# The new tokens' value product of the sample attention, contracted over 128 rows instead of 32

## What is computed

```python
def dilated_attention_sample(q, k_all, v_all, rel_bias):
    # q: (B,T,H,Dh) are the last T rows of k_all/v_all: (B,L,H,Dh)
...
    s = jnp.einsum('bthc,btkhc->bthk', q, kg)
    s = s * (HEAD_DIM ** -0.5) + bias.T[None, None]
    s = jnp.where(valid[None, :, None, :], s, NEG)
    p = jax.nn.softmax(s, axis=-1)
    return jnp.einsum('bthk,btkhc->bthc', p, vg)
```

## Time and profile before

| | us |
|---|---|
| median of 3 runs | 1195.9 (1193.57 to 1197.24) |
| span of the profiled execution, first to last instruction | 1191.4 |
| TensorE busy in it | 1134.9 (95%) |
| VectorE, ScalarE, GpSimd busy | 406.9, 323.6, 144.5 |
| share of the span on the chain that ended last | TensorE 85%, DMA 7%, VectorE 4% |

### The profile page before, as it was taken

How to read it: one execution, slowest core, us unless ns; L and a number is a source line. 1 busy time by engine, 2 the same in 40 slices (tenths; PEclk the granted TensorE clock), 3 DMA queues, 4 the chain that set the end, 5 groups by cost and what they waited for, 6 DMA issues and landing times.

```text
span 1191.4 us, 14847 instructions
## 1 busy us (share of the span) xinstructions
PE 1134.9 (95%) x5656; PEld 586.6 (49%) x5656; DVE 406.9 (34%) x968; ACT 323.6 (27%) x635; POOL 144.5 (12%) x141
## 2 busy tenths in 40 slices
PE   6999999899999999999999999899999988989997
PEld 3444443566666666655554555333443333334443
DVE  0232132556663242323256556362111111024443
ACT  2232231677741121110011111211111110134443
POOL 0110110011130000000011111321312210000000
PEclk9999999899999999999999999898999998989999
DMA  9211101311035525333568423799999999863421
GB/s 315 63 49 40 40 30 53 100 37 37 2 135 175 169 80 167 129 147 144 200 244 305 142 89 129 273 373 383 417 419 394 422 419 402 319 262 136 145 103 40
DMA packets 75061, 224.19 MB, mean 188 GB/s; under 512 B 18334, under 2 KB 32062, under 8 KB 60656
## 3 DMA queue, kind: packets, MB, share of 16 engines
q1 hardware_dynamic: 64384, 194.26, 44.0%
q0 software_dynamic: 9888, 26.37, 5.8%
q10 hardware_dynamic: 720, 2.62, 0.5%
HBM read 196.62 MB, written 31.32 MB: 191 GB/s over the span
## 4 chain that ended last, share of the span: by engine, by line
PE 85%; DMA 7%; DVE 4%; ACT 1%; issue 1%; POOL 0%; SPq 0%; ACTq 0%; POOLq 0%; DVEq 0%
PE pair L1915 14%; PE pair L2134 14%; PE pair L2331 11%; PE pair L2429 9%; PE pair L2197 9%; DMA R<-in_w_up 5%; PE pair L2353 4%; PE pair L1984 3%; PE pair L1971 3%; PE pair L1997 3%; PE pair L2226 1%; PE pair L2046 1%; PE pair L2318 1%; PE pair L2063 1%; PE pair L2050 1%
## 5 line engine op out<-in xcount | busy, mean ns | idle before, releaser
L2134 PE MATMUL pair<-R 128*128 128x352 f32 x576 | 180.8, 462 | 0.0
L1915 PE MATMUL pair<-R 128*128 128x512 f32 x384 | 172.0, 605 | 2.1 <-DMA R<-in_w_in 2.1
L2331 PE MATMUL pair<-R 128*32 128x512 f32 (+2 forms) x896 | 156.8, 628 | 11.2 <-DMA R<-in_w_up 9.2
L2134 PEld LDWEIGHTS pair<-R 128*128 128x128 f32 x576 | 105.3, 190 | 54.5 <-issue 4.4
L1915 PEld LDWEIGHTS pair<-R 128*128 128x128 f32 x384 | 73.3, 194 | 90.1 <-issue 90.1
L2429 PE MATMUL pair<-R 128*128 128x512 f32 x256 | 113.5, 601 | 1.7 <-issue 1.7
L2197 PE MATMUL pair<-R 128*128 128x512 f32 x256 | 113.8, 597 | 0.0
L2331 PEld LDWEIGHTS pair<-R 128*32 128x32 f32 (+2 forms) x896 | 50.0, 129 | 102.8 <-issue 98.5
L1736 DVE TENSOR_TENSOR R<-pair,R 128x256 f32<-128x256 f32 x21 | 8.9, 424 | 216.7 <-ACT R L1188 216.7
L2429 PEld LDWEIGHTS pair<-R 128*128 128x128 f32 x256 | 48.7, 193 | 60.7 <-issue 60.7
L2353 PE MATMUL pair<-R,bias 128*32 128x512 f32 (+2 forms) x448 | 76.4, 596 | 0.6 <-ACT bias L1192 0.6
(11 more groups left out here) (297 smaller groups left out, 1249.1 us busy)
## 6 DMA issues: line engine op xcount, KB each, us to landing
R<-in_w_gate SPq DMA_DIRECT2D x32, 1024.0 KB
R<-in_w_up SPq DMA_DIRECT2D x32, 1024.0 KB
R<-in_w_down SPq DMA_DIRECT2D x32, 1024.0 KB, 15.9
R<-in_x_prompt SPq DMA_DIRECT2D x16, 512.0 KB, 3.5
R<-in_cache_k SPq DMA_DIRECT2D x8, 1024.0 KB, 5.0
R<-in_cache_v SPq DMA_DIRECT2D x8, 1024.0 KB, 4.9
R<-y_dram SPq DMA_DIRECT2D x16, 512.0 KB, 6.7
R<-in_w_in SPq DMA_DIRECT2D x3, 2048.0 KB
```

Source lines behind the costliest of these rows:

```text
L1915: last = mm(bk[4 + part][0:n, :], xTs[a.u][:, c, 0:n], wA[:, c, AD * part:AD * part + AD], start=(c == 0), stop=(c == DC - 1))
L2134: last = mm(bk[b][:, 0:n], wB[q % 2][:, c, which, :], xT[:, c, lo:lo + n], start=(c == 0), stop=(c == DC - 1))
L2331: last = mm(bk[2 + u][r, :].rearrange("p (w f) -> p w f", w=2), xgT[u][:, c, r], wgu[s][:, :, c, :], start=(c == 0), stop=(c == DC - 1))
```

## The change

The last product of `weigh_values` contracts over all 128 rows. For that, the rows behind the 32 real ones must be zeros on one side and finite on the other: GpSimd clears the values' last tile at the start of the program, VectorE clears slot 7 of `PTs` once the prompt's attention is over, and two waits are adapted (`pool_set` counts one more). In the listing of the changed program every instruction behind the two new ones keeps its place and order on its engine.

```diff
@@ gpsimd, start of the program
         pool.memset(ones[:, :], 1.0).then_inc(S("pool_set"), 1)
         pool.memset(blank, 4 * TOK).then_inc(S("pool_set"), 1)
+        pool.memset(V[:, PT, :], 0.0).then_inc(S("pool_set"), 1)
@@ scalar, evac_qkv
             act.wait_ge(S("prj_full"), 3 * a.t + 3)
+            if n == SAMP:
+                act.wait_ge(S("pool_set"), 5)
             act.activation(V[0:n, a.t, :], bk[6][lo[2]:lo[2] + n, :], ACT.Copy).then_inc(S("prj_free"), 1)
@@ vector, keep_u
             if q == 0 and j == 0:
-                dve.wait_ge(S("pool_set"), 5)
+                dve.wait_ge(S("pool_set"), 6)
@@ vector, before the convolution
         dve.wait_ge(S("ot_full"), NSTEP)
         then(dve.memset(qbd, 0.0))
+        then(dve.memset(PTs[:, :, 7, :], 0.0))
         dve.wait_ge(S("qkT_done"), TILES)
@@ tensor, weigh_values
-            last = mm(bk[3][strips[3], :], rows(7, SAMP), V[0:SAMP, PT, :], start=False, stop=True)
+            last = mm(bk[3][strips[3], :], rows(7, P), V[:, PT, :], start=False, stop=True)
```

## The result

| | before | changed |
|---|---|---|
| median, us | 1193.57 (5 runs, 1189.19 to 1197.24) | 1184.05 (5 runs, 1180.12 to 1187.04) |
| ratio to before | 1 | 0.9921, 95% interval 0.9900 to 0.9943 |
| span of the profiled execution, us | 1191.4 | 1185.2 |
| TensorE busy in it, us | 1134.9 | 1125.6 |

The change makes the kernel faster by 0.79% (0.57 to 1.0%). The forecast was 0.65% and 1188.1 us.

The account below looks back on a forecast made before the run. TensorE's issued matmuls were taken to bound the kernel, busy 95% of the span. Eight calls at 0.97 us save 7.8 us, memsets and later stages cost nothing: 1195.9 - 7.8 = 1188.1 us, range 1184.5 to 1192.4.

Parts of the forecast that it names:

- The mechanism and its size: In `weigh_values`, the 128-row product starts beside the far products; each of eight calls saves 0.97 us, together 7.8 us.
- What was costed at nothing: GpSimd's memset at the start and VectorE's ahead of eight copies: hidden in idle time; uncovered, 0.6 and 0.1 to 0.7 us.
- the low bound of 0.1: VectorE's memset of 128 x 128: a quarter of 0.48 us is 0.1 us, at most 0.7.
- What so_full sets off: Loads after TensorE's calls stay in time: batch 7's values keep 22 us less 1.9, output weights 21.8 us.
- as argued: Experts' stage: its weight stream starts earlier by what TensorE gained, so the stage keeps its length and the gain isn't eaten.
- The step that failed: Final sum for the whole kernel: span 1191.4 - 7.8 = 1183.6 us; median kept 4.5 us above it, 1188.1.
- The lower end: Bottom of the forecast range for the whole kernel: 2.3 us of run spread and 1.3 us of clock below, 1184.5 us.
- The term of the saving: Eight calls of `weigh_values`, each 0.97 us shorter on TensorE: 7.8 us saved.
- The first, that the product does not join: In `weigh_values`, only one change of form goes, saving 0.8 us, time 1195.1 us; chance 7%.
- The second and third: Clock in the experts' stage: second, saving falls to 3.8 us, under 3.6 at 3%; third, over 3.6 us slower, 2%.

## Why the prediction was right about the change and wrong about the time

**The mechanism and its size were right.** Step by step: L2099 is 128*32 and starts with the far products, 0.02 us behind them (expected: within 0.05). A call takes 1.86 us in the timeline's rounding, 1.85 expected. From the first call to the last it is 117.12 us, 6.75 less than before (expected 6.8). The idle time ahead of its weight loads is gone. The stretch from the first call to the output projection is 7.7 us shorter, 8 x 0.97 = 7.8 expected. The form and the free strip were named as the two causes, and each was taken away alone: of the 0.97 us the form without the strip gives 0.13, the strip without the form nothing, and only both together give all.

**What was costed at nothing costs nothing that could be measured.** The memsets stand where expected, GpSimd's first and then VectorE's:

```profile
1.67 0.53 POOL L789 MEMSET R<- 128x512 f32 x1
10.74 1.03 POOL L793 COPY R<-R 128x1024 f32<-128x1024 f32 x1 [8.55 <-DVE R L1325]
```

```profile
349.77 0.17 DVE L1531 MEMSET R<- 128x128 f32 x1
...
356.56 0.18 DVE L1418 COPY R<-stT 128x16 f32<-128x16 f32 x1 [0.76 <-POOL R L834]
360.42 0.53 DVE L1422 TENSOR_TENSOR R<-pair,R 128x352 f32<-128x352 f32 x1 [3.68 <-PE pair L2138]
```

0.53 us of GpSimd's idle time and 0.17 us on VectorE, near the low bound of 0.1, with the same 0.76 and 3.68 us of idle time behind it as in the earlier trace rows. VectorE's stands at 349.8 instead of 346.9 us because everything from the projections on runs that much later in this execution. No wait of TensorE before the first score is new: the lines and what they wait for are those of before. Of the lengths the one that grew most, an idle time of 3.2 us at L1933 that was 1.8, is 3.2 in the kernel without the product and the memsets too.

**What so_full sets off stayed in time.** Batch 7's values and the output weights:

```profile
558.71 0.35 SPq L585 DMA_DIRECT2D R<-in_cache_v  x1
...
565.50 9.45 SPq L591 DMA_DIRECT2D R<-in_w_out  x8
```

From 558.71 to their first read at 578.87 it is 20.2 us (expected 22 - 1.9), from 565.50 to 587.27 21.8 us (expected 21.8). No wait came of it. Nothing shows that the experts' stage took any of the gain back, as argued: its length is 293.9 to 295.8 us in the changed traces, inside the 291.9 to 297.2 of before. Finer than that scatter the traces can't tell; the 8.1 us between the medians of 54 and 19 runs say that the gain arrived.

**The step that failed is the last one, "The median of the runs stands 4.5 us above the span; with that kept, it is 1195.9 - 7.8".** A run's time stands 1.8 us above its span, not 4.5: the profiled execution of the changed kernel has 1187.04 and a span of 1185.2, and the distance is 1.7 to 2.1 in every run of every kernel here. The 4.5 us that stand ahead of the prediction compared one execution's span with the median of others. So the profiled execution of before took some 1191.4 + 1.9 = 1193.3 us, and the three runs shown lay high in the kernel's scatter: 54 runs give 1192.8. From there the same saving leads to 1192.8 - 7.8 = 1185.0, against 1184.7 over 19 runs. Of the 4.05 us between forecast and measured median 3.1 are thus the base, 0.3 the saving (8.1 against 7.8) and 0.6 the luck of the five runs. The rest of the failure is the width: I took "2.3 us below and 1.3 above" of three runs for the scatter, where runs of before reach from 1187.7 to 1200.1. The lower end, 1188.1 - 2.3 - 1.3 = 1184.5, had no room for a high base and this scatter together, and 1184.05 falls 0.45 us outside. The term of the saving was right to 0.3 us.

**The rivals.** The first, that the product does not join, fell at once; the experiments on strip and rows show under which conditions it would have held. The second and third, a part or more given back, put the clock's scatter on the change; it exists, but in all kernels. The granted clock of the 54 runs of before goes from 0.974 to 0.987 and correlates with the time by -0.74; 0.001 of clock is worth 0.7 us. A share of the clock that moves like this between runs of one kernel belonged into the range, not into a rival.

## What to carry to other kernels

As far as these runs show it, for tiles of 128 x 32 in float32: products run side by side on TensorE when their tiles have the same form and stand on strips that are free. A small product of another form (32 x 32 and 64 x 32 were run) has the array to itself for all its passes, here 0.97 us instead of nothing, so filling it up with zeros to the form of its neighbours is cheap, once a strip is free and clearing costs no one's time. Count the products per strip first: eight over four strips, two on each, leave no gap. A change of form by itself is worth 0.1 us and does not pay for an order that takes away another engine's time to empty a bank. And before a forecast in absolute time: compare the profiled execution with the runs through the distance of its time and its span (1.7 to 2.1 us here), not through that of a median and a span; a median of three runs can lie 3 us off in a kernel that scatters by 1%.

## What the runs showed of the hardware that I had not expected

A 64 x 32 tile does not join 128 x 32 tiles any more than a 32 x 32 one: its 0.97 us are the same to 0.01.

Inside the changed stretch nothing scatters (133.23 us in six traces), while the stage bound by weight loads scatters by 5 us (291.9 to 297.2) in one kernel. Which stretch a change lies in decides how well a trace can weigh it; the runs' interval of 0.4% is that of the other stages.

The projections of the first tile wait for their weights 2.1 to 4.2 us, differing from one execution to the next, so the whole program starts up to 2 us later or earlier.

The granted clock can add a fixed amount in a fixed place or nothing: 1.7 us between the output projection and the router in seven of fourteen traces, 0.0 in the other seven.
